# Gate rows of the memory heads by transfers instead of TensorE products, and halves in the first attention

## The chip, the cores and the metric

The kernel runs on one core of a Trainium2 chip. The metric is the device time of one execution in microseconds (us). A core has TensorE (matrix products, PE in the profile), VectorE (DVE), ScalarE (ACT), GpSimd (POOL) and SyncE (SP, here only for transfers). They run side by side and are ordered by semaphores alone.

## The reference, cut to what matters

The program is a small hybrid model (two mixing layers, then a block of two feed-forward parts around a third mixer), for 256 tokens of width 1024, in float32. The change lies in the first layer. It has two branches: four memory heads (mLSTM) and an attention branch (NSA: compressed, selected and windowed keys). Of the memory heads, with `F` the running sum of the log forget gates, `i` the input gate, and `m` the running maximum of `i - F`:

```
a[s] = i[s] - F[s]
m[t] = max(0, max over s <= t of a[s])
S[s,t] = (k[s] . q[t]) * exp(a[s] - m[t])   for s <= t, else 0
h[t] = sum_s S[s,t] v[s] / max(|sum_s S[s,t]|, exp(-(F[t] + m[t])))
```

Each head needs `m[t]` and `F[t]+m[t]`, rows over the tokens `t`, on every one of the 128 partitions, which hold the keys `s`. Tokens are two blocks of 128: the tile for `s` in the first block has 256 columns, that for the second 128, so 384 per head. The attention has two kinds of softmax (`kind` 0 and 1) over the keys, in steps p = 0 to 7, each one block of 128 queries and one pair of heads; p = 4 to 7 have 256 keys.

## The kernel before

Weights come in units of 128 x 1024 numbers through a ring of four slots. SyncE loads a unit, ScalarE copies its high half (`whi`), GpSimd subtracts to get the low half (`wlo`), and TensorE makes 24 products of it (three for each of eight parts: `mm3`). The first layer (`even_in`) goes over 35 units `j`, on each engine in the same order, written out by hand; the small work of the branches stands between units. `ATT_AT` puts attention step `p` at units 18, 19, 20, 21, 22, 23, 25, 27, 28 (p = 0 to 8, where step p does the scores of p and the output of p-1); `ML_AT` puts the memory heads' steps m = 0 to 4 at units 29 to 33. Units 24 and 25, and 26 and 27, are pairs: TensorE does them together, and both end at once.

On ScalarE each unit is: drain of the unit's products where it owns them, `ahead` (wait until the unit is used, then the high half of the unit four later), then the small work. VectorE owns the other drains, and the convolution of units 15 to 22.

The steps that the change touches:

- `masks`: four small constant tiles, `before_bf` among them.
- `gate_maxima` (VectorE, unit 8) leaves `rows4` on four partitions, one for each head: row 2 is `m`, row 3 is `F+m`.
- `mlstm_front(h)` on TensorE: five products that spread the head's rows of `rows4` over all partitions (with a 4 x 128 selector from `pick`) and add 1e30 where `s > t` (with `before_bf`), in PSUM banks 5 and 4; then two query-key products in bank 6. `mlstm(m)` on ScalarE takes three exponentials of them, into `mem` and `mE`; on VectorE, `mlstm(m)` finishes head m-1 (maximum of `mad` and `mem`, reciprocal, product to `hm`) and then weights head m's scores into `mST` (its line in the profile is the helper's). `mlstm_back(h)` on TensorE multiplies `mST` with the values and with ones.
- `scores(p)` on TensorE makes both kinds; `score_maxima` on VectorE; exponentials in `attend` on ScalarE; the weighting of `prob` in `attend` on VectorE; `turned(p, turn)` on TensorE transposes the weights into bank 6, ScalarE copies them to `pt` (`weighted`), and `outputs` uses them. For p >= 4 there are two turns, one for each kind.

The profile shows the helpers' lines: L723 is every product, L2011 and L2020 the two forms of VectorE operations, L1493 every ScalarE function, L1573 the high halves, L658 GpSimd's low halves, L1011 the transposes of `turned`.

Of the kernel before, what the change touches and what calls it, by code (L numbers as in the profile page):

```python
# [16 lines left out]
F32 = mybir.dt.float32  # L17
# [7 lines left out]
P = 128  # L25
# [371 lines left out]
def program(nc, stream, vec_d, row_d, mat_d, cst_d, x_d, out_d):  # L397
    with ExitStack() as ctx:
# [40 lines left out]
        later_bf = sb("later_bf", [P, P], BF16)  # L439
        before_bf = sb("before_bf", [P, P], BF16)  # L440
        notyet_bf = sb("notyet_bf", [P, P], BF16)
# [3 lines left out]


        b1 = ExitStack()
        row = sb("row", [P, NROW], at=b1)
# [39 lines left out]
        flat_rs = rs[:].rearrange("p a b -> p (a b)")  # L488
        mE = flat_rs[:, 0:768].rearrange("p (w t) -> p w t", w=2)
        mST = flat_rs[:, 768:1536].rearrange("p (w t) -> p w t", w=2)  # L490
# [230 lines left out]
        def _(pe):  # L721
# [86 lines left out]
            def even_in():  # L808
# [5 lines left out]
                for j in range(2, E_UNITS):  # L814
# [8 lines left out]
                    if j in ATT_AT:  # L823
                        p = ATT_AT[j]
                        if j in CMP_AT:
                            scores(p)
                            turned(p - 1, 0)
                        else:
                            if p >= 1:
                                turned(p - 1, 0)  # L830
                            if p < 8:
                                scores(p)
                        if p >= 5:
                            turned(p - 1, 1)
                        if p >= 1:
                            outputs(p - 1)
# [86 lines left out]
            def mlstm_front(h):  # L923
                if h == 0:
                    pe.wait_ge(S("row_max"), 3)
                    pe.wait_ge(S("qk_ready"), 2)
                    pe.wait_ge(S("att_pt"), 12)
                else:
                    pe.wait_ge(S("mlstm_st"), h)
                one = C("pick", 512, 4)[:, h * P:(h + 1) * P]  # L930
                mm(ps[:, 5, 0:T], one, rows4[:, 2, :], True, False)
                mm(ps[:, 5, 0:P], ident_bf[:], before_bf[:], False, True)
                mm(ps[:, 5, T:T + P], one, rows4[:, 2, P:T], True, False)
                mm(ps[:, 5, T:T + P], ident_bf[:], before_bf[:], False, True)
                mm(ps[:, 4, 0:T], one, rows4[:, 3, :])
                mm(ps[:, 6, 0:T], qk[:, 4 + h, 0:P], qk[:, h, :])
                mm(ps[:, 6, T:T + P], qk[:, 4 + h, P:T], qk[:, h, P:T]).then_inc(S("mlstm_s"), 1)
# [41 lines left out]

            def scores(p):  # L980
                qt, i = p // 4, p % 4
                nk = P * (qt + 1)
                if p == 0:
                    pe.wait_ge(S("rope_done"), 6)
                    pe.wait_ge(S("masks"), 4)
                else:
                    pe.wait_ge(S("att_exp"), 4 * p)
                for kind in range(2):
                    o = kind * T
                    for g in range(2):  # L990
                        mm(ps[:, 4 + g, o:o + nk], nqk[64 * g:64 * g + 64, i, qt * P:(qt + 1) * P],
                           nqk[64 * g:64 * g + 64, 4 + kind, 0:nk], True, False)
                    for g in range(2):
                        m = mm(ps[:, 4 + g, o + nk - P:o + nk], ident_bf[:], later_bf[:], False, True)
                m.then_inc(S("att_s"), 1)

# [6 lines left out]
            def turned(p, turn):  # L1003
                t = p if p < 4 else 4 + 2 * (p - 4) + turn
                pe.wait_ge(S("att_p"), p + 1)
                if t:
                    pe.wait_ge(S("att_pt"), t)
                if t <= 2:
                    pe.wait_ge(S("cmp_tc"), t // 2 + 1)
                for n, (kind, st, g) in enumerate(blocks(p, turn)):  # L1010
                    m = nc.tensor.transpose(ps[:, 6, n * P:(n + 1) * P],  # L1011
                                            prob[:, p % 2, g, kind * T + st * P:kind * T + (st + 1) * P], C("ident"))
# [476 lines left out]
        def _(act):  # L1489
# [99 lines left out]
            def even_in():  # L1589
# [5 lines left out]
                for j in range(4):  # L1595
                    dst[E_NZ + j] = nz[:, j, :]
                between = {3: (masks,), 5: (forget_log,), 8: (queries_sq,), 10: (queries_rs, hidden), 12: (by_feature,),
                           13: (second_layer, log_table), 14: (kc_rs, gates)}
                for j in range(E_UNITS):
# [17 lines left out]
                    if last:  # L1617
                        weighted(8, 1)
                    elif j in ATT_AT:
                        attend(ATT_AT[j])  # L1620
                    if j == 25:
                        act.wait_ge(S("drained_v"), drained("v", G_E + E_QK + 7))
# [34 lines left out]
            def masks():  # L1657
                act.wait_ge(S("consts_in"), 64)
                func(ident_bf[:], C("ident"), ACT.Copy, "masks")
                func(before_bf[:], C("gt"), ACT.Copy, "masks", scale=BIG)  # L1660
                func(notyet_bf[:], C("nge"), ACT.Copy, "masks", scale=BIG)
# [36 lines left out]
            def forget_log():  # L1698
# [4 lines left out]
                func(ps[:, 7, 64:72], gl[:, 1, :], ACT.Ln, "log1p", bias=eps[:, 2:3])  # L1703

            def log_table():
                nc.scalar.preload_act_table_set(LOG_EXP)
# [6 lines left out]
            def mlstm(m):  # L1713
                if m >= 1:
# [3 lines left out]
                    func(mad[:, (m - 1) % 2, :], ps[:, 7, T:2 * T], ACT.Abs, "mlstm_d")  # L1718
                if m < 4:
                    act.wait_ge(S("mlstm_s"), m + 1)  # L1720
                    if m >= 2:
                        act.wait_ge(S("mlstm_st"), m - 1)
                    func(mem[:, m, :], ps[:, 4, 0:T], ACT.Exp, scale=-1.0)
                    func(mE[:, m % 2, 0:T], ps[:, 5, 0:T], ACT.Exp, scale=-1.0, bias=gl[:, 5, m:m + 1])
                    func(mE[:, m % 2, T:T + P], ps[:, 5, T:T + P], ACT.Exp, "mlstm_e", scale=-1.0,
                         bias=gl[:, 5, 4 + m:5 + m])

            def weighted(p, turn):
                t = p - 1 if p <= 4 else 4 + 2 * (p - 5) + turn
                act.wait_ge(S("att_tr"), t + 1)  # L1730
                if t >= 2:
                    act.wait_ge(S("att_av"), t - 1 if t < 6 else 4 + (t - 4) // 2)
                func(pt[:, t % 2, :], ps[:, 6, :], ACT.Copy, "att_pt")

# [272 lines left out]
        def _(dve):  # L2007
# [97 lines left out]
            def even_in():  # L2105
                between = {4: (small_columns,), 5: (forget,), 6: (gate_columns,), 8: (gate_maxima, compress), 10: (normalized, hidden),
                           11: (rotated,), 14: (kc_n,), 15: (kc_rot,), 18: (compressed,)}
                for j in range(E_UNITS):
# [13 lines left out]
                    if j == 16:  # L2122
                        gated()
                    if j == 27:
                        dve.wait_ge(*once("qk_th"))
# [41 lines left out]
            def gate_maxima():  # L2167
# [3 lines left out]
                step(nc.vector.tensor_tensor_scan(rows4[:, 2, :], rows4[:, 1, :], rows4[:, 1, :], 0.0, ALU.max, ALU.max), "row_max")  # L2171
                tt(rows4[:, 3, :], rows4[:, 2, :], ps[0:4, 4, 0:T], ALU.add, "row_max")

            def normalized():
# [51 lines left out]
            def mlstm(m):  # L2226
# [6 lines left out]
                if m < 4:  # L2233
                    dve.wait_ge(S("mlstm_e"), m + 1)

                    stt(mST[:, m % 2, :], ps[:, 6, 0:384], 0.25 * P ** -0.5, mE[:, m % 2, :], ALU.mult, ALU.mult, "mlstm_st")

# [31 lines left out]
            def attend(p):  # L2269
# [8 lines left out]
                if p < 8:  # L2278
# [5 lines left out]
                    nk = P * (qt + 1)  # L2284
                    weights = prob[:, p % 2].rearrange("p g (k n) -> p (g k) n", k=2)[:, :, 0:nk]
                    tt(weights, weights, end(r, nk), ALU.mult, "att_p")

# [446 lines left out]
```

## Time and profile before

| | us |
|---|---|
| median of 3 runs | 994.34 |
| lowest, highest | 993.43, 994.58 |
| the profiled execution | 993.42 |
| its span in the profile | 991.6 |
| TensorE busy | 938.4 (95%) |
| VectorE busy | 481.5 (49%) |
| ScalarE busy | 535.9 (54%) |
| GpSimd busy | 628.5 (63%) |
| chain that ended last: TensorE's share | 57% |

The span is from the first to the last instruction; the rest of the execution's time lies around it. Busy shares are averages over stages with different limits, so the table of stages and the timelines say more. A row's bracket at its end says how long the engine had stood idle before it and what ended that.

### The profile page before, as it was taken

The page shows a single profiled execution, that of the slowest core. Times are in us where ns is not written, and L with a number is a line of the kernel's source. Part 1 is how long each engine was busy: PE and PEld are TensorE (multiplying, and loading weights), DVE is VectorE, ACT ScalarE, POOL GpSimd, SP SyncE. Part 2 cuts the span into 40 slices and gives each one's busy share as a digit, 9 for nine tenths or more (in the row PEclk, how much of TensorE's full clock was granted, in tenths as well). Part 3 has the DMA queues.
Part 4 walks back from the last instruction along what each step waited for, and adds up shares of the span by engine and source line. Part 5 has one row for each costly group of instructions (what it writes and reads, how often), then busy time and mean ns, then how long its engine had stood idle before and what let it go on. Part 6 is the DMA issues. An engine that isn't in the chain of part 4 may idle for free.

```text
span 991.6 us, 24182 instructions
## 1 busy us (share of the span) xinstructions
PE 938.4 (95%) x9548; PEld 894.6 (90%) x9548; DVE 481.5 (49%) x865; ACT 535.9 (54%) x795; POOL 628.5 (63%) x266
## 2 busy tenths in 40 slices
PE   5999989999888789999999999999999999999997
PEld 4988777899888779999999989999988999999996
DVE  5256534785789764433331133663574743333112
ACT  6577654666945776444443346776322654554441
POOL 2885334377797237977778846654413679788882
PEclk9999999999989999999999999999999999999999
DMA  9644223254434314655555534332002346555551
GB/s 344 205 159 149 73 77 104 67 171 142 159 127 130 128 43 154 210 174 181 172 170 172 180 116 149 128 129 86 3 4 88 118 160 201 183 188 189 180 184 43
DMA packets 39046, 139.86 MB, mean 141 GB/s; under 512 B 4272, under 2 KB 5552, under 8 KB 38832
## 3 DMA queue, kind: packets, MB, share of 16 engines
q1 hardware_dynamic: 38960, 138.62, 42.0%
q8 instruction: 66, 1.08, 0.5%
q14 instruction: 20, 0.16, 0.1%
HBM read 137.55 MB, written 1.05 MB: 140 GB/s over the span
## 4 chain that ended last, share of the span: by engine, by line
PE 57%; issue 9%; DVE 9%; POOL 6%; ACT 4%; POOLq 0%; DVEq 0%; ACTq 0%
PE ps L723 57%; POOL wlo L658 5%; ACT ps L1493 1%; DVE wlo L2011 1%; DVE hA L2439 1%; ACT whi L1573 1%; DVE qkl L2011 1%; DVE ps L2011 1%; POOL rN L699 1%; DVE aL L2020 0%; DVE mad L2011 0%; DVE hT L2047 0%; DVE ivt L2020 0%; POOL dif L682 0%; DVE mixT L2020 0%
## 5 line engine op out<-in xcount | busy, mean ns | idle before, releaser
L658 POOL TENSOR_TENSOR wlo<-ring,whi 128x1024 fp32r<-128x1024 f32 x243 | 585.6, 2424 | 312.7 <-ACT whi L1573 294.6
L1573 ACT ACTIVATE whi<-ring 128x1024 fp32r<-128x1024 f32 x253 | 266.6, 1060 | 204.9 <-PE ps L723 184.7
L723 PE MATMUL ps<-aH,whi 128*128 128x272 f32 (+1 forms) x1048 | 306.6, 293 | 6.1 <-DVE aL L2057 4.9
L723 PE MATMUL ps<-aH,wlo 128*128 128x272 f32 (+1 forms) x1048 | 300.6, 287 | 0.0
L723 PE MATMUL ps<-aL,whi 128*128 128x272 f32 (+1 forms) x1048 | 300.0, 286 | 0.0
L723 PEld LDWEIGHTS ps<-aH,whi 128*128 128x128 f32 x1048 | 199.4, 190 | 11.5 <-DVE wlo L2011 4.8
L723 PEld LDWEIGHTS ps<-aL,whi 128*128 128x128 f32 x1048 | 199.4, 190 | 0.6 <-issue 0.5
L723 PEld LDWEIGHTS ps<-aH,wlo 128*128 128x128 f32 x1048 | 199.4, 190 | 0.0
L723 PE MATMUL ps<-fxH,whi 128*128 128x256 f32 x480 | 135.6, 283 | 3.3 <-DVE fxL L2011 1.8
L723 PE MATMUL ps<-fxL,whi 128*128 128x256 f32 x480 | 135.0, 281 | 0.0
L723 PE MATMUL ps<-fxH,wlo 128*128 128x256 f32 x480 | 135.0, 281 | 0.0
L723 PE MATMUL ps<-fH,wlo 128*128 128x272 f32 (+1 forms) x352 | 100.3, 285 | 0.0
L723 PE MATMUL ps<-fH,whi 128*128 128x272 f32 (+1 forms) x352 | 100.0, 284 | 0.0
L723 PE MATMUL ps<-fL,whi 128*128 128x272 f32 (+1 forms) x352 | 100.0, 284 | 0.0
L723 PEld LDWEIGHTS ps<-fxH,whi 128*128 128x128 f32 x480 | 90.7, 189 | 5.0 <-DVE fxL L2011 2.5
L723 PEld LDWEIGHTS ps<-fxH,wlo 128*128 128x128 f32 x480 | 90.8, 189 | 0.0
L723 PEld LDWEIGHTS ps<-fxL,whi 128*128 128x128 f32 x480 | 90.2, 188 | 0.1
L2011 DVE TENSOR_TENSOR ps<-ps,rstd 128x256 f32<-128x256 f32 (+1 forms) x35 | 15.3, 436 | 113.8 <-PE ps L723 109.4
L723 PEld LDWEIGHTS ps<-fH,whi 128*128 128x128 f32 x352 | 66.3, 188 | 0.0
L723 PEld LDWEIGHTS ps<-fL,whi 128*128 128x128 f32 x352 | 66.2, 188 | 0.0
L723 PEld LDWEIGHTS ps<-fH,wlo 128*128 128x128 f32 x352 | 66.2, 188 | 0.0
L2504 DVE TENSOR_TENSOR ps<-ps,rstd 128x272 f32<-128x272 f32 (+1 forms) x44 | 19.4, 441 | 57.7 <-PE ps L723 48.4
(377 smaller groups left out, 1380.5 us busy)
## 6 DMA issues: line engine op xcount, KB each, us to landing
ring<-in_stream SPq DMA_DIRECT2D x253, 512.0 KB, 3.3
cst<-in_cst SPq DMA_DIRECT2D x1, 1325.0 KB, 12.7
xT<-in_x SPq DMA_DIRECT2D x4, 272.0 KB, 3.5
out<-hT SPq DMA_DIRECT2D x4, 256.0 KB, 2.4
row<-in_row SPq DMA_DIRECT2D x1, 898.0 KB, 9.2
cst<-in_cst SPq DMA_DIRECT2D x1, 640.0 KB, 10.2
mat<-in_mat SPq DMA_DIRECT2D x1, 576.0 KB, 13.5
vec<-in_vec SPq DMA_DIRECT2D x1, 135.0 KB, 3.7
```

The lines of the kernel that those rows point to most:

```text
L658: nc.gpsimd.tensor_tensor(wlo[:, s, :], ring[:, s, :], whi[:, s, :].bitcast(F32), ALU.subtract).then_inc(S("w_split"), 1)
L699: nc.gpsimd.tensor_tensor(rN[:, li % 2], rN0[:], m.unsqueeze(1).broadcast_to([P, 17, 64]), ALU.mult).then_inc(S("r_n"), 1)
L723: return nc.tensor.matmul(out, lhsT, rhs, start=start, stop=stop, skip_group_check=True)
L1493: step(nc.scalar.activation(out, in_, f, **kw), sem)
L1573: nc.scalar.activation(whi[:, v % SLOTS, :], ring[:, v % SLOTS, :], ACT.Copy).then_inc(S("w_high"), 1)
L2011: step(nc.vector.tensor_tensor(out, a, b, op), sem)
L2439: step(nc.vector.copy_predicated(out, m.broadcast_to([P, 8, P // (2 * b), b]).bitcast(U32), src), "lev_a")
L2504: nc.vector.tensor_tensor(gate, gate, rstd[:, 0:TT - c0], ALU.mult).then_inc(S("ffn_gate"), 1)
```

## The change

Row 2 and row 3 of `rows4` are written to a tensor in the chip's memory by one transfer at unit 11, and read back at unit 15 by five transfers that repeat each row on all 128 partitions: into `mE` (now two tiles of two heads each, one in `rs`, one in `mixT`) and `mem`. All six are issued by ScalarE. The 1e30 of the mask is added on VectorE by `masked_rows` at unit 24, for all four heads. The exponentials of `mem` (one for all heads) and of heads 0 and 1 are at unit 26, those of heads 2 and 3 in memory steps 0 and 1. The five gate products of each head go, and `before_bf` with them.

In the attention, steps 5 to 7 make the scores of kind 0, then the first transposes of the step before, then the scores of kind 1. VectorE weights the kinds one after the other for p >= 4, and each turn of transposes waits for its own kind only. The last transposes use bank 4.

```diff
+        rows_d = nc.dram_tensor("gate_rows_d", (4, 2, T), F32).ap()
-        mE = flat_rs[:, 0:768].rearrange("p (w t) -> p w t", w=2)
+        mE = [t[:, 0:768].rearrange("p (w t) -> p w t", w=2) for t in (flat_rs, mixT[:].rearrange("p a b -> p (a b)"))]
...
+                        elif 5 <= p < 8:
+                            scores(p, (0,))
+                            turned(p - 1, 0)
+                            scores(p, (1,))
...
-                one = C("pick", 512, 4)[:, h * P:(h + 1) * P]
-                mm(ps[:, 5, 0:T], one, rows4[:, 2, :], True, False)
-                mm(ps[:, 5, 0:P], ident_bf[:], before_bf[:], False, True)
-                mm(ps[:, 5, T:T + P], one, rows4[:, 2, P:T], True, False)
-                mm(ps[:, 5, T:T + P], ident_bf[:], before_bf[:], False, True)
-                mm(ps[:, 4, 0:T], one, rows4[:, 3, :])
...
-                pe.wait_ge(S("att_p"), p + 1)
-                if t:
+                pe.wait_ge(S("att_p"), t + 1)
+                if t and t < 11:
                     pe.wait_ge(S("att_pt"), t)
...
-                    m = nc.tensor.transpose(ps[:, 6, n * P:(n + 1) * P],
+                    m = nc.tensor.transpose(ps[:, 6 if t < 11 else 4, n * P:(n + 1) * P],
...
+                    if j == 26:
+                        func(mem[:], mem[:], ACT.Exp, scale=-1.0)
+                        for h in range(2):
+                            gate_powers(h)
...
-                func(before_bf[:], C("gt"), ACT.Copy, "masks", scale=BIG)
...
+            def rows_out():
+
+                act.wait_ge(S("row_max"), 3)
+                nc.scalar.dma_start(rows_d, rows4[:, 2:4, :]).then_inc(S("rows_out"), 16)
+
+            def rows_in():
+
+                act.wait_ge(S("rows_out"), 16)
+                def row(what, h0, n, t0):
+                    return rows_d[h0:h0 + n, what, t0:T].unsqueeze(0).broadcast_to([P, n, T - t0])
+                for i in range(2):
+                    nc.scalar.dma_start(mE[i][:, :, 0:T], row(0, 2 * i, 2, 0)).then_inc(S("rows_in"), 16)
+                    nc.scalar.dma_start(mE[i][:, :, T:T + P], row(0, 2 * i, 2, P)).then_inc(S("rows_in"), 16)
+                nc.scalar.dma_start(mem[:], row(1, 0, 4, 0)).then_inc(S("rows_in"), 16)
+
+            def gate_powers(h):
+
+                act.wait_ge(S("rows_masked"), h + 1)
+                e = mE[h // 2][:, h % 2, :]
+                func(e[:, 0:T], e[:, 0:T], ACT.Exp, scale=-1.0, bias=gl[:, 5, h:h + 1])
+                func(e[:, T:T + P], e[:, T:T + P], ACT.Exp, "mlstm_e", scale=-1.0, bias=gl[:, 5, 4 + h:5 + h])
...
-                if m < 4:
-                    act.wait_ge(S("mlstm_s"), m + 1)
-                    if m >= 2:
-                        act.wait_ge(S("mlstm_st"), m - 1)
-                    func(mem[:, m, :], ps[:, 4, 0:T], ACT.Exp, scale=-1.0)
-                    func(mE[:, m % 2, 0:T], ps[:, 5, 0:T], ACT.Exp, scale=-1.0, bias=gl[:, 5, m:m + 1])
-                    func(mE[:, m % 2, T:T + P], ps[:, 5, T:T + P], ACT.Exp, "mlstm_e", scale=-1.0,
-                         bias=gl[:, 5, 4 + m:5 + m])
+                if m < 2:
+                    gate_powers(m + 2)
...
+                    if j == 24:
+                        masked_rows()
...
+            def masked_rows():
+
+                dve.wait_ge(S("rows_in"), 80)
+                for h in range(4):
+                    e = mE[h // 2][:, h % 2, :].rearrange("p (b t) -> p b t", t=P)[:, 0::2, :]
+                    stt(e, mid(C("gt"), 2), BIG, e, ALU.mult, ALU.add, "rows_masked")
...
                     dve.wait_ge(S("mlstm_e"), m + 1)
-
-                    stt(mST[:, m % 2, :], ps[:, 6, 0:384], 0.25 * P ** -0.5, mE[:, m % 2, :], ALU.mult, ALU.mult, "mlstm_st")
+                    dve.wait_ge(S("mlstm_s"), m + 1)
+                    stt(mST[:, m % 2, :], ps[:, 6, 0:384], 0.25 * P ** -0.5, mE[m // 2][:, m % 2, :], ALU.mult, ALU.mult, "mlstm_st")
...
-                    weights = prob[:, p % 2].rearrange("p g (k n) -> p (g k) n", k=2)[:, :, 0:nk]
-                    tt(weights, weights, end(r, nk), ALU.mult, "att_p")
+                    if p < 4:
+                        weights = prob[:, p % 2].rearrange("p g (k n) -> p (g k) n", k=2)[:, :, 0:nk]
+                        tt(weights, weights, end(r, nk), ALU.mult, "att_p")
+                    else:
+                        for kind in range(2):
+                            weights = prob[:, p % 2, :, kind * T:kind * T + nk]
+                            tt(weights, weights, end(r2[:, :, kind], nk), ALU.mult, "att_p")
```

## Rows read from the trace of the kernel before

**Rows 1.** Stages: window, us, then busy us of PE, PEld, DVE, ACT, POOL.
```profile
135.50:161.10 25.60, 23.17 (x207) 18.75 (x205) 10.61 (x17) 15.23 (x29) 11.76 (x5) 1.00 0.27 87
161.10:188.80 27.70, 26.85 (x169) 21.89 (x168) 15.37 (x13) 14.09 (x28) 9.42 (x4) 1.00 0.28 92
```
**Rows 2.** TensorE's timeline, memory heads: start, us, what, idle before.
```profile
161.10 0.69 PE L723 MATMUL ps<-rows,cst 4*128 4x256 f32 x2
...
163.08 0.92 PE L723 MATMUL ps<-qk 128*128 128x256 f32 x4
163.76 0.36 PE L723 MATMUL ps<-aH,whi 128*128 128x256 f32 x1
...
166.64 0.82 PE L723 MATMUL ps<-rs,vtok 128*128 128x256 f32 x4
...
174.06 0.92 PE L723 MATMUL ps<-rs,vtok 128*128 128x256 f32 x4 [0.30 <-DVE rs L2020]
...
188.84 0.92 PE L723 MATMUL ps<-rs,vtok 128*128 128x256 f32 x4 [0.59 <-DVE rs L2020]
```
**Rows 3.** ScalarE's timeline, memory heads.
```profile
164.46 0.88 ACT L1493 ACTIVATE rs<-ps,gl 128x256 f32<-128x256 f32 x2
```
**Rows 4.** VectorE's timeline, memory heads.
```profile
168.84 2.33 DVE L2011 TENSOR_TENSOR mad<-mad,mem 128x256 f32<-128x256 f32 x1 [2.85 <-ACT mad L1493]
...
192.75 0.42 DVE L2011 TENSOR_TENSOR mad<-mad,mem 128x256 f32<-128x256 f32 x1
```
**Rows 5.** GpSimd's timeline, attention and memory heads.
```profile
136.90 4.70 POOL L658 TENSOR_TENSOR wlo<-ring,whi 128x1024 fp32r<-128x1024 f32 x2 [9.01 <-ACT whi L1573]
...
168.54 2.35 POOL L658 TENSOR_TENSOR wlo<-ring,whi 128x1024 fp32r<-128x1024 f32 x1 [3.25 <-ACT whi L1573]
```
**Rows 6.** L2020 by operands (minimum/median/maximum ns), and VectorE's timeline.
```profile
L2020 DVE SCALAR_TENSOR_TENSOR fQ<-fQ,mixT x5: 424/426/1812, 262.3 to 268.6; 128x256 f32<-128x256 f32 x5
...
84.93 1.52 DVE L2020 SCALAR_TENSOR_TENSOR qk<-ps,vec,qk 128x253 f32<-128x253 f32 x3
86.48 1.41 DVE L2020 SCALAR_TENSOR_TENSOR nz<-th,nz 128x1024 f32<-128x1024 f32 x1
```
**Rows 7.** TensorE's timeline, attention.
```profile
95.74 1.05 PE L977 MATMUL ps<-cst,pc 128*15 128x128 f32 x8 [2.30 <-DVE pc L2011]
...
125.60 0.66 PE L1011 MATMUL ps<-cst,prob 128*128 128x128 f32 x4 [1.80 <-DVE prob L2011]
...
127.04 0.70 PE L723 MATMUL ps<-nqk 64*128 64x256 f32 x4
...
149.01 0.63 PE L1011 MATMUL ps<-cst,prob 128*128 128x128 f32 x4 [0.58 <-ACT pt L1493]
```
**Rows 8.** VectorE's timeline, attention.
```profile
90.94 1.78 DVE L2011 TENSOR_TENSOR pc<-pc,cs 128x240 f32<-128x240 f32 x1
...
124.32 1.22 DVE L2011 TENSOR_TENSOR prob<-prob,pst 128x1024 f32<-128x1024 f32 x1
...
135.78 0.89 DVE L2011 TENSOR_TENSOR vtok<-ps,row 128x256 f32<-128x256 f32 x2 [2.30 <-PE ps L723]
137.92 1.22 DVE L2267 TENSOR_REDUCE pst<-ps 128x4 f32<-128x1024 f32 x1 [1.25 <-PE ps L723]
```
**Rows 9.** ScalarE's timeline, attention.
```profile
81.86 0.43 ACT L1493 ACTIVATE ps<-ps,vec 128x256 f32<-128x256 f32 x1
...
142.13 1.92 ACT L1493 ACTIVATE th<-qk 128x2048 f32<-128x2048 f32 x1
146.38 2.00 ACT L1573 ACTIVATE whi<-ring 128x1024 fp32r<-128x1024 f32 x2 [2.33 <-PE ps L723]
148.29 0.58 ACT L1493 ACTIVATE pt<-ps 128x512 f32<-128x512 f32 x1
...
150.36 0.47 ACT L1493 ACTIVATE prob<-ps,pst 128x256 f32<-128x256 f32 x1
```
**Rows 10.** SyncE's timeline: DMA issues at the start.
```profile
0.75 1.82 SPq L616 DMA_DIRECT2D xT<-in_x  x4
```

More of the change, by code:

```diff
@@ L439, in program @@
         later_bf = sb("later_bf", [P, P], BF16)
-        before_bf = sb("before_bf", [P, P], BF16)
         notyet_bf = sb("notyet_bf", [P, P], BF16)
@@ L924, in mlstm_front @@
                 if h == 0:
-                    pe.wait_ge(S("row_max"), 3)
                     pe.wait_ge(S("qk_ready"), 2)
@@ L978, in compressed_rows, with scores @@
                 m.then_inc(S("cmp_t"), 1)
-            def scores(p):
+            def scores(p, kinds=(0, 1)):
                 qt, i = p // 4, p % 4
@@ L984, in scores @@
                     pe.wait_ge(S("rope_done"), 6)
-                    pe.wait_ge(S("masks"), 4)
+                    pe.wait_ge(S("masks"), 3)
                 else:
                     pe.wait_ge(S("att_exp"), 4 * p)
-                for kind in range(2):
+                for kind in kinds:
                     o = kind * T
@@ L994, in scores @@
                         m = mm(ps[:, 4 + g, o + nk - P:o + nk], ident_bf[:], later_bf[:], False, True)
-                m.then_inc(S("att_s"), 1)
+                if kinds[-1] == 1:
+                    m.then_inc(S("att_s"), 1)
             def blocks(p, turn):
@@ L1597, in even_in @@
                 between = {3: (masks,), 5: (forget_log,), 8: (queries_sq,), 10: (queries_rs, hidden), 12: (by_feature,),
-                           13: (second_layer, log_table), 14: (kc_rs, gates)}
+                           13: (second_layer, log_table), 14: (kc_rs, gates), 11: (rows_out,), 15: (rows_in,)}
                 for j in range(E_UNITS):
@@ L1732, in weighted @@
                     act.wait_ge(S("att_av"), t - 1 if t < 6 else 4 + (t - 4) // 2)
-                func(pt[:, t % 2, :], ps[:, 6, :], ACT.Copy, "att_pt")
+                func(pt[:, t % 2, :], ps[:, 6 if t < 11 else 4, :], ACT.Copy, "att_pt")
             def attend(p):
```

## The prediction

> **What bounds the kernel now.** I read the table of stages first, then TensorE's own timeline in the two stages that the change touches, then ScalarE, VectorE and GpSimd in the same stretches. TensorE is busy nearly all the time, so a removed product is worth something only if nothing else then becomes late. The table shows two places that matter: attention, from 135.50 to 161.10, where TensorE is busy 23.17 of 25.60 us, and the memory heads, 161.10 to 188.80, 26.85 of 27.70 us [rows 1]. Outside the first layer nothing is edited, and the weight ring has only four slots, so time gained or lost here is neither stored nor spent later: the layer's change is the kernel's change.
>
> In the memory stage the reader is to see a loop. For each head TensorE does one front (gate products and query-key products), one projection unit and the back of the head before. One front runs from 161.10 to 163.76, of which the part before 163.08 (1.98 us) is the five gate products; the unit runs from 163.76 to 166.64 [rows 2]. Beside it runs a chain through ScalarE, VectorE and back: ScalarE's absolute value, the maximum at 168.84 (2.33 us), then 2.9 us for reciprocal, product and weighting, and the next back at 174.06 [rows 2, 4]. TensorE waits only 0.30 and 0.59 us at the backs of 174.06 and 188.84 [rows 2]: chain and products are almost equally long.
>
> The 2.33 us of that maximum is not its work: the same 256 columns take 0.42 us at 192.75 [rows 4]. GpSimd's subtraction runs from 168.54 for 2.35 us, and the maximum ends as it ends [rows 4, 5]. VectorE operations with two operands in SBUF stand still behind a GpSimd subtraction that began earlier. fQ's row says the same: 424 ns at best, 1812 at worst for one shape, an addition-and-product form (the one that masked_rows uses) [rows 6]. The Trainium skill (SBUF — State Buffer, "Who interferes with whom") says that a VectorE instruction with two SBUF inputs and a GpSimd one that reads SBUF exclude each other for the whole instruction. By that rule, the trace agrees.
>
> **Memory stage.** Removed: five gate products in each of four heads, 4 x 1.98 = 7.9 us of TensorE [rows 2]; three exponentials per head move out of the loop, two of them (0.88 us, [rows 3]) staying at heads 2 and 3. If TensorE alone set the pace, the gain would be 7.9. It doesn't. Count from the first front, F = 161.10. The front is now 0.68, the unit 2.88, so the unit ends at F+3.56. ScalarE does drain, high half and absolute value behind it as before; from the unit's end (166.64) to the next back (174.06) the old trace takes 7.42 us [rows 2], because GpSimd's subtraction again comes 0.3 us before the maximum. Back 1: F+10.98 (before F+12.96).
> Next head: that back takes 1.5 (1.40 from 166.64 to the front behind it, and a restart after the wait), the front 0.68, the unit ends at F+16.04. GpSimd's subtraction was started by the unit that ended at F+8.52; with the 1.90 us between 166.64 and 168.54 [rows 2, 5] it runs F+10.4 to 12.75, and the maximum asks 0.6 after the back's end, at F+13.06: free, 0.42 instead of 2.33. Then 2.9: back 2 at F+16.38, with TensorE idle 0.3.
> Third: the subtraction F+17.9 to 20.3 comes before the maximum's request at F+18.46, so it is blocked again: back 3 at F+23.46, against 188.84 - 161.10 = 27.74 before [rows 2]. Gain 4.3 us; the rest of the 7.9 turns into waits of TensorE at backs 1, 2, 3 of some 2.4, 0.3 and 2.0 us, where it waited 0.30 and 0.59 before. Bounds: 7.9 if the chain were never in the way; 2.4 if the second maximum is blocked too (1.9 more). I take 4.3, the count from the rows. What follows (four low halves, the last head, squares) keeps its distance from back 3 to 0.2 us.
>
> **First split head (p=5).** Before, transposes at 125.60 waited 1.80 for the weights [rows 7]. The weighting started 124.32 and took 1.22 in one [rows 8]; in halves the first is done 0.53 sooner. The first kind of the next scores now lies in the wait; before, it ran behind the transposes, which with it take 1.44, 0.66 of them the transposes [rows 7], so 0.8 is hidden. Sum: 1.3 us sooner. At p=6 and 7 TensorE does not wait for the weights, so the split gives nothing; at p=8 the next transpose goes to a free bank, but ScalarE's high half still lies between its two copies: 0.05.
>
> **masked_rows at p=6.** It stands on VectorE behind the pair's drain (135.78 + 0.89 = 136.67) and ahead of the score maximum that started at 137.92 [rows 8]. Four additions over two SBUF operands, 256 columns each, some 0.45 with the gap (fQ's 424 ns, [rows 6]). The first is in before GpSimd's subtractions (136.90, two in 4.70 [rows 5]). The second waits out one subtraction, the third the other, since each side gets the port when the other's instruction ends. Relative to U = 135.51: done at U+7.6 instead of U+3.1. The score maximum goes from U+2.4 to U+7.6, the exponentials end at U+11.3.
> Behind them on ScalarE are the tanh of 2048 columns (1.92, [rows 9]), then the high half at 146.38, and now, before the next high half and before the copy that the transposes of p=7 wait for (149.01, [rows 7]), the new exponentials: one of 1024 columns (1.0, half of the tanh's 2048) and two pairs at 0.88 [rows 3], with gaps 2.9 us. The copy, before at 148.29, comes at U+18.15; the second transposes at U+18.85 (before U+13.5); then the exponentials of p=7 at U+20.2, before 150.36 = U+14.85 [rows 9]: 5.35 later. The first half of the weights gives 0.55 back, and attention ends 4.8 later, net of the 1.3 above 3.5. Bounds: 0 if ScalarE hid everything (excluded: the copy is in order behind them and TensorE already waits 0.58 for it [rows 7]); 2.3 if the additions never stand behind GpSimd; 4.8. I take 4.8, since rows 4 and 6 both show the block.
>
> **The transfers (j=11 and 15).** One write and five broadcasts, all issued by ScalarE. The trace has no issue from ScalarE; on SyncE four take 1.82, 0.46 each [rows 10]. Five are 2.3 to 3.0 us, during which ScalarE's next bias (81.86, [rows 9]) waits; the high half at 80.89 covers 0.96. So it is 1.4 to 2.0 late. VectorE takes that unit at 84.93 [rows 6], 2.05 us after ScalarE has it ready (a scaling of like width behind the bias), which would hide it, but the high half behind it is late too, so GpSimd's subtraction now starts at about 85.7 and stands before the gate product at 86.48, which in this trace slipped in between two of them [rows 6]. I get 1.1 to 1.9 later at the subtraction of 90.94, on which TensorE waits 2.30 at 95.74 [rows 8, 7]. Bounds: 0 (issues under 0.2 us, or over 0.52, where the product again comes first) and 1.9. I take 1.5. The data are 1.3 MB in a stretch where the transfer engines are not the limit and are wanted 50 us later: nothing. The write at j=11 lies in a wait of ScalarE; one mask copy less at j=3 as well: nothing, and TensorE has no wait there.
> The Trainium skill (DMA: Bandwidth & Descriptors, "Issuing engines are not separate DMA queues") calls the issue time on the sequencer usually small relative to the transfer. Read as nothing, that gives a sum 1.5 lower. Here SyncE's rows show 0.46 for a 512 KB load that lands in 3.3, small but not free.
>
> **Sum.** -4.3 (memory) -1.3 (p=5) +4.8 (p=6, 7) +1.5 (issues) = +0.7, less 0.05: +0.6 us. The profiled run was 993.42 (span 991.6, 1.8 around it), 0.9 under the median of 994.34; the change is taken on the median: 994.9.
>
> **Rivals.**
> 1. The additions of masked_rows do not stand behind GpSimd. For: only some of the two-operand rows are slow. Against: rows 4 and 6. Then -1.9 us; 992.5, just at the bound of 0.2%. With issues free as well -3.4: 991.0.
> 2. The memory loop is not held by the maximum, because a shift of 0.5 us makes VectorE's request come first at back 3 or at back 1. Each takes 1.9 off: one gives -1.3, both -3.2 (991.1). For: requests are only 0.3 and 0.5 us apart. Against: at 168.84 the order is set by one engine, ScalarE's high half, then its absolute value.
> 3. Slower: ScalarE's issues are dear. The broadcasts have 256 to 512 rows each. From 1.2 us each (6.0 in all), ScalarE is 5.0 late, 3.0 beyond the cover of 2.05, and the compressed scores with it: +3.0 in place of 1.5, sum +2.1, 996.4; at 1.5 us each +3.6. Against: SyncE's 0.46. That the second maximum is blocked too (+1.9, sum +2.5) ends on the same side.
> 4. The change does not do what it says: the products are gone for certain; only their worth is in question.
>
> **Chances.** Forecast: 0.38, within 0.2% (2.0 us, about what a measurement of this kernel can tell from no change). Rival 1: 0.22, of which 0.12 beyond that bound (with cheap issues). Rival 2: 0.18, of which 0.12 beyond (both backs). Rival 3 with its companion: 0.22, all slower. So faster 0.24, same 0.38 + 0.10 + 0.06 = 0.54, slower 0.22. The range is from 990.8 (rivals 1 or 2 at their best) to 997.3 (rival 3 between 1.2 and 1.5 us).
>
> **What would show it.** In the changed profile: backs of the memory heads 5.4 to 7.4 us apart, maxima of 2.3, 0.42, 2.3 us, and TensorE waits of about 2 us for VectorE; masked_rows' additions of 2 us and more, and the score maximum of p=6 some 5 us later in its unit; a TensorE wait of about 4 us (not 0.58) for the pt copy in p=7; the wait of 1.80 in p=5 gone; the wait of 2.30 at the compressed rows grown to about 3.8. I am wrong if the additions take 0.5 each, if the copy in p=7 is on time, or if three maxima of 0.42 follow each other.

## The result and the profile after

The changed kernel takes 999.85 us (median of 6 runs, 997.05 to 1002.62), the kernel before, run beside it, 994.03 (992.07 to 994.75). The ratio is 1.0060, with a 95% interval of 1.0041 to 1.0078: slower by 5.8 us, outside the range of 990.8 to 997.3. The profiled execution is one of the fastest (997.05, span 995.2); its mean granted clock is 0.984, against 0.992 before. It is only 3.6 us longer than the profiled execution of the kernel before (993.42), where the medians are 5.8 apart; the two traces speak for the first of these differences.

TensorE's timeline of the changed kernel (the rows that answer to [rows 2, 7]):

```profile
97.70 1.05 PE L974 MATMUL ps<-cst,pc 128*15 128x128 f32 x8 [2.10 <-DVE pc L2028]
...
127.06 0.66 PE L1009 MATMUL ps<-cst,prob 128*128 128x128 f32 x4 [0.29 <-DVE prob L2028]
...
136.32 0.70 PE L723 MATMUL ps<-nqk 64*128 64x256 f32 x4
...
154.67 1.09 PE L1009 MATMUL ps<-cst,prob 128*128 128x128 f32 x4 [4.88 <-ACT pt L1491]
...
169.38 0.82 PE L723 MATMUL ps<-qk 128*128 128x256 f32 x4
...
180.35 0.92 PE L723 MATMUL ps<-rs,vtok 128*128 128x256 f32 x4 [2.51 <-DVE rs L2037]
...
185.77 0.92 PE L723 MATMUL ps<-rs,vtok 128*128 128x256 f32 x4 [0.34 <-DVE rs L2037]
...
192.72 1.53 PE L723 MATMUL ps<-rs,vtok 128*128 128x256 f32 x4 [1.88 <-DVE rs L2037]
```

Apart from the first row, the waits are where the prediction put them. But the duration in the second column is to be read too: the four transposes at 154.67 take 1.09 us where those of 149.01 took 0.63 [rows 7], and the back at 192.72 takes 1.53 where that of 188.84 took 0.92 [rows 2]. The same instructions run slower. The table of windows (us; busy us of PE, PEld, DVE, ACT, POOL; then TensorE's granted clock) says why; first the kernel before, then the changed one:

```profile
152.00:162.00 10.00, 8.73 (x74) 7.14 (x73) 4.31 (x6) 4.00 (x10) 2.58 (x2) 1.00 0.37 123
```

```profile
152.00:162.00 10.00, 7.33 (x41) 6.37 (x42) 3.22 (x6) 5.30 (x13) 2.84 (x2) 0.50 0.35 107
162.00:169.00 7.00, 6.07 (x57) 5.25 (x57) 1.54 (x3) 2.61 (x4) 2.37 (x1) 0.99 0.04 4
...
192.70:196.00 3.30, 3.28 (x12) 2.93 (x13) 3.23 (x3) 0.40 (x2) 2.22 (x1) 0.53 0.02 5
```

For ten microseconds TensorE was granted half its speed: 0.50 is the lower of its two levels, 1.2 GHz in place of 2.4. Before that it had stood still for 4.88 us. At the third back, behind waits of 2.51, 0.34 and 1.88 us, a shorter slow stretch comes (0.53).

A third slow stretch is hidden; it is the first in time. The wait at the compressed rows was to grow from 2.30 to about 3.8 and is 2.10, though the rows themselves are late. The products ahead of it ran slowly, so TensorE came late too; the same table, one microsecond to the row:

```profile
89.00:90.00 1.00, 1.00 (x18) 1.00 (x17) 0.96 (x2) 0.97 (x2) 1.00 (x1) 1.00 1.05 392
...
91.00:92.00 1.00, 1.00 (x9) 0.78 (x8) 0.90 (x4) 0.00 (x0) 1.00 (x1) 0.50 0.74 291
92.00:93.00 1.00, 1.00 (x6) 1.00 (x6) 0.90 (x4) 0.00 (x0) 1.00 (x2) 0.50 0.21 86
```

The last product ahead of the wait begins at 95.31 here and at 93.16 before: 2.15 later, of which 0.67 came with it. Without the slow stretch the wait would have been 3.6. This one cost nothing, because TensorE had to wait for VectorE there anyway, and the stage behind it is as long as in the kernel with the attention's halves alone, where no such stretch lies ahead (38.6 us from the compressed rows to the first product behind the pair before p=6).

Reading off when the same piece of work starts in both traces gives the ledger. The shift of a row is its start after less its start before; the last column is what the stage added.

| up to | before | after | shift | this stage | forecast |
|---|---|---|---|---|---|
| ScalarE's high half ahead of the issues | 80.89 | 81.56 | +0.67 | +0.67 | 0 |
| compressed rows | 95.74 | 97.70 | +1.96 | +1.29 | +1.5 |
| first product behind the pair before p=6 | 135.51 | 136.32 | +0.81 | -1.15 | -1.3 |
| first memory front | 161.10 | 169.38 | +8.28 | +7.47 | +4.8 |
| third back | 188.84 | 192.72 | +3.88 | -4.40 | -4.3 |
| sums of squares of the next norm | 224.95 | 230.46 | +5.51 | +1.63 | 0 |
| end of the span | 991.6 | 995.2 | +3.6 | -1.9 | 0 |

The first line isn't the work of the transfers: the kernel with the attention's halves alone, which changes nothing ahead of that row, has it at 81.42. The last line lies in code that the change does not touch, and is the clock's for the most part: the kernel before has slow stretches there for some 13.6 us in all (an estimate from rows of 1 us: at 272, 336 and 603 us), the changed kernel for some 10.2 (at 278 and 329), which is up to 1.7 us of work.

VectorE and GpSimd at unit 24, where masked_rows stands (they answer to [rows 5, 8]):

```profile
136.50 0.88 DVE L2028 TENSOR_TENSOR vtok<-ps,row 128x256 f32<-128x256 f32 x2 [2.22 <-PE ps L723]
137.42 2.92 DVE L2037 SCALAR_TENSOR_TENSOR rs<-cst,rs 128x256 f32<-128x256 f32 x2
140.37 2.95 DVE L2037 SCALAR_TENSOR_TENSOR mixT<-cst,mixT 128x256 f32<-128x256 f32 x2
143.36 1.22 DVE L2293 TENSOR_REDUCE pst<-ps 128x4 f32<-128x1024 f32 x1
...
137.62 4.96 POOL L658 TENSOR_TENSOR wlo<-ring,whi 128x1024 fp32r<-128x1024 f32 x2 [7.67 <-ACT whi L1571]
```

Four additions take 5.9 us; away from GpSimd's subtractions they take 1.8 (the second experiment below). The score maximum comes 7.04 after the pair's end (136.32) instead of 2.41. ScalarE behind it:

```profile
147.06 1.91 ACT L1491 ACTIVATE th<-qk 128x2048 f32<-128x2048 f32 x1
149.00 1.06 ACT L1571 ACTIVATE whi<-ring 128x1024 fp32r<-128x1024 f32 x1
149.97 1.04 ACT L1491 ACTIVATE mem<-mem 128x1024 f32<-128x1024 f32 x1
151.04 1.92 ACT L1491 ACTIVATE rs<-rs,gl 128x256 f32<-128x256 f32 x4
152.99 1.06 ACT L1571 ACTIVATE whi<-ring 128x1024 fp32r<-128x1024 f32 x1
153.95 0.58 ACT L1491 ACTIVATE pt<-ps 128x512 f32<-128x512 f32 x1
```

The copy to pt comes at 153.95, 17.63 after the pair's end (counted: 18.15). And the five issues on ScalarE's queue, after which its next bias starts at 84.20, not 81.86 [rows 9]:

```profile
81.57 0.40 ACTq L1717 DMA_DIRECT2D rs<-gate_rows_d  x1
82.00 0.48 ACTq L1718 DMA_DIRECT2D rs<-gate_rows_d  x1
82.51 0.60 ACTq L1717 DMA_DIRECT2D mixT<-gate_rows_d  x1
83.14 0.49 ACTq L1718 DMA_DIRECT2D mixT<-gate_rows_d  x1
83.66 0.49 ACTq L1719 DMA_DIRECT2D mem<-gate_rows_d  x1
84.20 0.45 ACT L1491 ACTIVATE ps<-ps,vec 128x256 f32<-128x256 f32 x1 [1.57 <-issue]
```

The product on nz, 1.41 us before [rows 6], now stands behind a subtraction for 2.73 us (start 87.14).

In the memory heads, VectorE's three maxima (they answer to [rows 4]) are blocked, free and blocked, as forecast:

```profile
175.08 2.38 DVE L2028 TENSOR_TENSOR mad<-mad,mem 128x256 f32<-128x256 f32 x1 [4.18 <-ACT mad L1491]
...
182.45 0.43 DVE L2028 TENSOR_TENSOR mad<-mad,mem 128x256 f32<-128x256 f32 x1 [2.15 <-ACT mad L1491]
...
187.87 1.96 DVE L2028 TENSOR_TENSOR mad<-mad,mem 128x256 f32<-128x256 f32 x1 [2.15 <-ACT mad L1491]
```

### The profile page after: what moved, and what is told of

Read it like the earlier page. It is cut to its first block, busy times and chain, and to the rows that moved or that the text cites. A ratio compares the mean times of both kernels' runs of the same rounds, so it can differ in the third digit from the quotient of the medians.

```text
span 995.2 us, 24128 instructions
## 1 busy us (share of the span) xinstructions
PE 934.6 (94%) x9516; PEld 893.6 (90%) x9516; DVE 489.3 (49%) x873; ACT 534.9 (54%) x791; POOL 627.8 (63%) x266
## 4 chain that ended last, share of the span: by engine, by line
PE 57%; issue 9%; DVE 8%; POOL 6%; ACT 4%; POOLq 0%; ACTq 0%; DVEq 0%
PE ps L723 57%; POOL wlo L658 5%; ACT ps L1491 1%; DVE wlo L2028 1%; ACT whi L1571 1%; DVE hA L2470 1%; DVE mad L2257 1%; POOL rN L699 0%; DVE qkl L2028 0%; DVE aL L2037 0%; DVE ps L2028 0%; DVE mad L2028 0%; DVE hT L2064 0%; DVE ivt L2037 0%; POOL dif L682 0%
```

## The experiments

Every time is compared with runs of the kernel before on the same chip, so ratios are compared with ratios; the changed kernel's own, 1.0060, is the mark.

**Is the loss the clock's? TensorE kept at work in p=7.**

```diff
+                            if p == 7:
+                                for _ in range(7):
+                                    mm(ps[:, 0, 0:432], C("ones"), cst[:, 0:432])
```

> The changed kernel with seven products of 432 columns (about 0.7 us each, result unused, into a free bank) put into TensorE's stream at p=7, where it otherwise stands still for 4.88 us. No other work moves. Clock theory: TensorE is granted half speed from about 151 to 162 because it stood still; kept at work it keeps full speed, the outputs of p=6, unit 28 and the last transposes take their old times, and the time falls by 2 to 3 us (to about 997). Queue theory (the loss is only the late copy from ScalarE): the fillers end when the copy comes, nothing changes, 999.9, within 0.5.

Measured: 995.85 us (10 runs), ratio 1.0023 (1.0004 to 1.0042), some 3.7 us less than the changed kernel's ratio gives. Added work made the kernel faster. TensorE's timeline of this kernel:

```profile
152.96 5.29 PE L723 MATMUL ps<-cst 128*128 128x432 f32 x14
158.09 0.60 PE L1012 MATMUL ps<-cst,prob 128*128 128x128 f32 x4
158.98 1.10 PE L723 MATMUL ps<-pt,vsw 128*64 128x128 f32 x16
```

Its windows:

```profile
158.00:170.00 12.00, 11.29 (x104) 9.57 (x104) 4.75 (x8) 5.69 (x14) 4.73 (x2) 1.00 0.22 74
...
97.00:101.00 4.00, 3.50 (x18) 2.17 (x18) 3.68 (x9) 2.73 (x6) 0.00 (x0) 0.53 0.00 1
101.00:104.00 3.00, 2.93 (x20) 1.85 (x18) 1.34 (x3) 2.10 (x6) 2.34 (x1) 0.50 0.00 0
```

The copy still comes late (157.28, which is 17.62 after the pair's end at 139.66; 17.63 in the changed kernel), but behind it the transposes take 0.60 and the outputs 1.10, at a granted clock of 1.00. From the pair's end to the first memory front it is now 29.86 us, against 33.06 in the changed kernel and 25.59 before. So the clock costs 3.2 us in this stage, and all the rest of the change 4.27. In this execution a slow stretch lies at 97 to 104 us, where the changed kernel's trace shows 1.00 on the same code: how an execution is clocked there varies. The waits at the backs are as in the changed kernel (2.51, 0.35 and 1.88 us), but the third back takes 0.92 and no slow stretch follows; from there to the sums of squares it is 36.16 us, as before (36.11), against 37.74 in the changed kernel.

**Each suspected place by itself.** masked_rows at unit 21, the exponentials at unit 28, the issues at unit 18:

```diff
-                    if j == 24:
+                    if j == 21:
                         masked_rows()
```

> The changed kernel with masked_rows at the end of unit 21 instead of unit 24, where VectorE has 1.8 us without work and GpSimd rests. If the additions behind GpSimd's subtractions make p=6 late: they take 0.45 each, the score maximum of p=6 comes 5.2 us earlier, TensorE's wait in p=7 falls from 4.88 to about 3.5 us (ScalarE's exponentials at unit 26 remain), a gain of 2 to 2.4 us, and up to 2.7 more if the shorter wait keeps the clock. If ScalarE's exponentials alone hold p=7, the wait stays near 4.9 and the gain is under 0.5.

```diff
-                    if j == 26:
+                    if j == 28:
+                        act.wait_ge(S("rows_in"), 80)
                         func(mem[:], mem[:], ACT.Exp, scale=-1.0)
                         for h in range(2):
                             gate_powers(h)
```

> The changed kernel with the exponentials of mem and of heads 0 and 1 at the end of unit 28 instead of unit 26, in a stretch where ScalarE waits 3.8 us. masked_rows stays at unit 24. If the exponentials in the queue before the copy cost what I counted: TensorE's wait in p=7 falls from 4.88 to about 2.1 us, a gain of 2.6 to 2.9 us, and up to 2.7 more with the clock. If the late score maximum alone holds p=7: the wait stays, gain under 0.5.

```diff
-                           13: (second_layer, log_table), 14: (kc_rs, gates), 11: (rows_out,), 15: (rows_in,)}
+                           13: (second_layer, log_table), 14: (kc_rs, gates), 11: (rows_out,), 18: (rows_in,)}
```

> The changed kernel with the five broadcast transfers issued at unit 18 instead of unit 15, where ScalarE waits 3.6 us for VectorE. If the issues delay GpSimd's subtraction and with it the product on nz (2.73 us instead of 1.41) and the compressed scores: 1.2 us less before 97.7, time 1.2 lower, unless a slow stretch of the clock moves. If the issues were covered: no change, within 0.5.

Measured: 998.94 (ratio 1.0057, 1.0037 to 1.0077), 996.10 (1.0024, 1.0012 to 1.0036) and 996.97 (1.0037, 1.0025 to 1.0049). The waits in TensorE's timelines, first with masked_rows at unit 21, then with the exponentials at 28, then with the issues at 18:

```profile
153.66 1.09 PE L1009 MATMUL ps<-cst,prob 128*128 128x128 f32 x4 [3.61 <-ACT pt L1491]
```

```profile
151.20 0.92 PE L1009 MATMUL ps<-cst,prob 128*128 128x128 f32 x4 [1.84 <-ACT pt L1491]
```

```profile
96.36 1.04 PE L974 MATMUL ps<-cst,pc 128*15 128x128 f32 x8 [0.76 <-DVE pc L2028]
```

The waits moved as counted: 4.88 to 3.61 and to 1.84 in p=7, and 2.10 to 0.76 at the compressed rows. The additions at unit 21 took 0.89 and 0.88 us for two each. The times did not follow the waits one to one. With masked_rows early the ratio falls by 0.0003 only, where 2 us (0.0020) were expected: the two intervals are wide enough for that, but my number missed. Its trace shows where the gain went. From the pair's end (137.25) to the first memory front (167.66) it is 2.6 us shorter than in the changed kernel, somewhat more than expected, though the transposes after the wait of 3.61 us are still slow (1.09). But from there to the third back it is 24.92 us instead of 23.34: a slow stretch at 180 to 184 (granted clock 0.58) lies behind the first back, and the third waits 2.49 us. With the exponentials at 28 the gain is 3.6 us by the ratios. The clock falls there behind a wait of only 1.84 us (transposes 0.92, granted clock 0.53 from 151 to 158), for a shorter time. The issues at 18 gave 2.3 us by the ratios where 1.2 was due; the product on nz is back at 1.41 us.

**Both places of the attention, then the issues too.** The first kernel has masked_rows at 21 and the exponentials at 28, the second has the issues at 18 as well:

> masked_rows at unit 21 and the three exponential groups at unit 28 together. If these two places are all that the attention loses: TensorE's wait in p=7 is back at 0.6 us, no slow stretch of the clock follows it, the first memory front comes 7.5 us earlier than in the changed kernel relative to p=5, the memory heads keep their gain of 4.4, and the time is 990 to 991.5, some 3 us under the kernel before. If a third thing holds p=7, a wait of over 1.5 us stays and the time is over 993.

> As the one before, with the five transfers issued at unit 18 as well. My count gives 1.3 us less than with the issues at unit 15 (wait at the compressed rows 0.76 instead of 2.1), 989 to 990. A rival that says the early stage is hidden in the end gives no difference between the two.

Measured: 992.90 (0.9993, 0.9978 to 1.0007) and 989.63 (0.9951, 0.9936 to 0.9967). The wait in p=7 is 0.57 us in both, as before the change, and the transposes after it take 0.63: no third thing holds p=7. But the first is 1.5 to 3 us over what I expected, and TensorE's timeline of it shows one reason in the memory heads:

```profile
173.01 1.65 PE L723 MATMUL ps<-rs,vtok 128*128 128x256 f32 x4 [2.51 <-DVE rs L2038]
...
186.91 0.92 PE L723 MATMUL ps<-rs,vtok 128*128 128x256 f32 x4 [2.06 <-DVE rs L2038]
```

The back after 2.51 us of standing still takes 1.65 instead of 0.92. The second kernel has the time that was expected. Its profiled execution is the slowest of its eight (994.07), and the wait at the compressed rows is 2.27 there, not 0.76: no slow stretch lies ahead of it (1.00 from 90 to 94), and one lies behind it (0.52 from 97 to 107).

**The maximum behind GpSimd.** The absolute value goes to PSUM, so the maximum has one operand in SBUF. Once on top of the kernel before this one, once alone on the changed kernel:

```diff
-                    func(mad[:, (m - 1) % 2, :], ps[:, 7, T:2 * T], ACT.Abs, "mlstm_d")
+                    func(ps[:, 5, (m - 1) % 2 * T:(m - 1) % 2 * T + T], ps[:, 7, T:2 * T], ACT.Abs, "mlstm_d")
...
-                    tt(d, d, mem[:, m - 1, :], ALU.max)
+                    tt(d, ps[:, 5, (m - 1) % 2 * T:(m - 1) % 2 * T + T], mem[:, m - 1, :], ALU.max)
```

> As the one before, and ScalarE writes the absolute value of each head's denominator into PSUM (bank 5, now free) instead of SBUF, so that VectorE's maximum has only one operand in SBUF. If the maximum of 2.33 us is a wait for GpSimd's subtraction, it takes 0.45 in every head, TensorE's waits of 2.5 and 1.9 us at backs 1 and 3 fall below 0.6, the rest of the 7.9 us comes in (3 to 3.5 more), no slow stretch of the clock follows, and the time is 985 to 987. If VectorE's chain is long for another reason, the maximum stays at 2.3 and the time stays at 989 to 990.

> The changed kernel with nothing but the absolute value in PSUM. If the maximum behind GpSimd's subtraction is what ate the rest of the 7.9 us in the memory heads: backs 5.4 us apart throughout, 3 to 3.5 us less, and up to 1.7 more because the slow stretch that follows the wait at back 3 is not entered: 995 to 997 against 999.9. p=7 keeps its wait of 4.9 and its slow stretch. If the lock is not it: 999.9.

Measured: 983.76 (4 runs; 0.9907, 0.9875 to 0.9938) and 994.30 (12 runs; 0.9998, 0.9986 to 1.0011). VectorE's and TensorE's timelines of the kernel with all four edits:

```profile
165.27 0.43 DVE L2029 TENSOR_TENSOR mad<-ps,mem 128x256 f32<-128x256 f32 x1 [4.19 <-ACT ps L1491]
...
170.68 0.42 DVE L2029 TENSOR_TENSOR mad<-ps,mem 128x256 f32<-128x256 f32 x1 [2.14 <-ACT ps L1491]
...
176.08 0.43 DVE L2029 TENSOR_TENSOR mad<-ps,mem 128x256 f32<-128x256 f32 x1 [2.14 <-ACT ps L1491]
```

```profile
168.59 0.92 PE L723 MATMUL ps<-rs,vtok 128*128 128x256 f32 x4 [0.56 <-DVE rs L2038]
173.99 0.92 PE L723 MATMUL ps<-rs,vtok 128*128 128x256 f32 x4 [0.33 <-DVE rs L2038]
179.39 0.92 PE L723 MATMUL ps<-rs,vtok 128*128 128x256 f32 x4 [0.33 <-DVE rs L2038]
```

And one of GpSimd's subtractions in it:

```profile
164.97 2.40 POOL L658 TENSOR_TENSOR wlo<-ring,whi 128x1024 fp32r<-128x1024 f32 x1 [1.11 <-ACT whi L1571]
```

Three maxima of 0.42 to 0.43, backs 5.4 apart, TensorE waiting 0.3 to 0.6 us. Each maximum begins and ends inside a subtraction (the other two start at 169.77 and 175.40), and none is held by it. The wait of 2.33 us was GpSimd's. Alone on the changed kernel the edit gives 5.5 us by the medians and 6.2 by the ratios, though its trace has p=7 unmended (wait 4.88, transposes 1.09); 3.5 of them were counted as the waits that vanish. The slow stretch at the third back, which cost the changed kernel 1.6 us (the tail's line in the ledger), does not occur in this trace: its granted clock from 163 to 196 us is 1.00. But one trace doesn't stand for twelve runs. Their mean granted clock is 0.983, the same as that of the changed kernel's six, so the clock as a whole was no better, and 2 to 2.7 us of this gain stay unexplained.

**The two parts of the change.** The kernel before with the halves alone, and the best kernel without the halves:

> The kernel before with only the attention part of the change (scores and weights of p=4 to 7 in halves, last transposes in bank 4). My count: the wait of 1.80 us at p=5 shrinks to 0.3, 1.2 us less, nothing elsewhere: 992.3 against 993.6. Rival, that the halves lose their gain at the next ScalarE copies: within 0.3 of the kernel before.

> The best kernel so far (gate rows by transfers, issues at unit 18, masked_rows at unit 21, exponentials at unit 28, maximum from PSUM) without the attention's halves. The halves alone gave 2.7 us on the kernel before, where my count says 1.2. If the parts add: 985 to 986.5 against 983.8. If the halves' gain was partly chance of the clock: 984.5 to 985.

Measured: 990.97 (10 runs; 0.9969, 0.9954 to 0.9983) and 985.63 (0.9919, 0.9905 to 0.9932). The halves are worth 3.1 us on the kernel before (2.7 by the medians) and, by the ratios, 1.2 on the best kernel, of which four runs leave an interval of some 3 us either way. In both the wait at p=5 is what changes (1.80 to 0.29, and 1.91 to 0.28), 1.5 us. The rest of the 3.1 isn't in any stage of the first layer's timeline. The mean granted clock of the ten runs is 0.993, against 0.9915 in the 23 runs of the kernel before beside them; the difference is up to 1.4 us of TensorE's work (0.0014 of 990 us, an estimate), about what is missing. Whether the halves bring that about or chance does isn't shown. The gate rows with their three mended places and the maximum are worth 0.81%, 8 us.

**The control: stand still without the change.** On the kernel before, four exponentials whose result nobody uses, ahead of the copy in p=7; then the same with six unused products on TensorE:

```diff
+                    if j == 26:
+                        for _ in range(4):
+                            func(mem[:], nz[:], ACT.Exp, scale=-1.0)
```

```diff
+                        if p == 7:
+                            for _ in range(6):
+                                mm(ps[:, 0, 0:432], C("ones"), cst[:, 0:432])
```

> The kernel before with four exponentials of 1024 columns (about 1.07 us each, result unused) on ScalarE at unit 26, ahead of the copy that the second transposes of p=7 wait for. It lengthens that wait of TensorE from 0.58 to about 4.9 us and changes nothing else. Queue alone: 3.8 to 4.3 us slower, 997.4 to 998. Clock theory: in most executions a slow stretch of 3.4 to 10.2 us follows as well, 1.7 to 5 us more: 999 to 1001.

> The same, with six products of 432 columns (about 0.7 us each, result unused) in TensorE's stream where it would stand still. Queue alone: the same time as without them, within 0.5. Clock theory: no slow stretch after p=7, 1.5 to 3 us faster than without them, 997 to 998.

Measured: 1001.98 (1.0082, 1.0065 to 1.0099) and 997.02 (1.0036, 1.0023 to 1.0049), 5 us apart. TensorE's timeline and one row of the windows of the first:

```profile
153.49 1.09 PE L1011 MATMUL ps<-cst,prob 128*128 128x128 f32 x4 [4.93 <-ACT pt L1493]
```

```profile
156.00:160.00 4.00, 4.00 (x26) 3.67 (x23) 2.44 (x5) 1.58 (x6) 0.00 (x0) 0.51 0.41 135
```

And of the second:

```profile
148.48 4.57 PE L723 MATMUL ps<-cst 128*128 128x432 f32 x12
153.58 0.63 PE L1014 MATMUL ps<-cst,prob 128*128 128x128 f32 x4 [0.53 <-ACT pt L1496]
```

```profile
156.00:160.00 4.00, 3.26 (x27) 2.82 (x25) 2.52 (x5) 1.87 (x7) 0.00 (x0) 1.00 0.38 131
```

The copy comes equally late in both (transposes at 153.49 and 153.58). What differs is whether TensorE stood still in front of it. Against the kernel before, a copy that comes 4.4 us later costs 3 to 3.6 us where TensorE is kept at work, and 4.6 to 5 more where it stands still (by the ratios and by the medians). That is more than the 1.5 to 3 expected. The two traces show 3.8 of it: from these transposes to the first memory front's query-key products the first kernel takes 2.2 us longer, and from there to the first back 1.6, in a second slow stretch (0.50 at 171 to 173) ahead of which TensorE had stood still for no more than 0.91 us. Whether the first stretch brings on the second isn't shown.

## Why the prediction was wrong

The list of mechanisms was right and most of their sizes were. What was missing is a term.

- Memory heads, "gain 4.3": measured 4.40, with backs at F+10.97, 16.39 and 23.34 against 10.98, 16.38 and 23.46 counted, and maxima blocked, free, blocked.
- p=5, "1.3 us sooner": 1.15. Transfers, "I take 1.5": 1.29, from five issues of 0.40 to 0.60 us. The sign that I gave for it, the wait "grown to about 3.8", did not show, because TensorE came late for the reason told above. Rival 3 (dear issues) falls with these rows.
- masked_rows behind GpSimd: 5.9 us for the four additions against 6.4 counted (1.2 to 7.6); rival 1 falls. The copy in p=7 came 17.63 after the pair's end, counted 18.15.
- The step that failed is the sum of that part, "attention ends 4.8 later": it is 7.47. The copy came even earlier than counted; what follows it was costed at durations from full clock, and between 152 and 162 TensorE ran at half. With the clock kept by unused products the same part is 4.27, so the queues were even a little overcounted (by 0.5) and the clock's term, put at nothing, is 3.2. The prediction had noted a wait of over 4 us on TensorE and asked only what was late next, not what it does to TensorE's own speed. The same omission stands in "keeps its distance from back 3 to 0.2 us": measured 1.63 more, after the waits that the prediction itself had listed (2.4, 0.3, 2.0). Together 4.3 us are missing (2.67 and 1.63): with them the sum of +0.6 is +4.9, near the measured 5.8 (+5.51 in the traces, up to the next norm).
- That idleness is the cause is shown for p=7, the larger part: the unused products take the slow stretch away in the changed kernel (1.0060 to 1.0023) and in the control (1.0082 to 1.0036), with the copy as late as without them. For the 1.63 behind the third back it isn't shown. The slow stretch is seen there, but in two other traces the same waits (2.51, 0.34 or 0.35, and 1.88 us) are followed by full clock (unused products in p=7, and exponentials at unit 28), and nobody kept TensorE at work at the backs.
- The range was made from queue effects of both signs and could not hold this: a cost that only adds, wherever a gap on TensorE is long.

The record gives the mean granted clock of every run. Within a kernel, the runs with the lower clock are by and large the longer ones. A thousandth of it is 2 us at half speed, so up to 1 us of TensorE's work (an estimate).

| kernel | runs | mean granted clock |
|---|---|---|
| before (three groups) | 25, 23, 20 | 0.991 to 0.992 |
| changed | 6 | 0.983 (slowest run 0.978, the two fastest 0.984 and 0.987) |
| changed, unused products in p=7 | 10 | 0.989 |
| changed, masked_rows at 21 | 5 | 0.981 |
| both places moved | 10 | 0.985 |
| maximum from PSUM alone on the changed kernel | 12 | 0.983 |
| all four edits | 4 | 0.990 |
| before with the halves alone | 10 | 0.993 |
| before, copy late | 6 | 0.986 |
| before, copy late, unused products | 8 | 0.992 |

What stays open: what starts the slow stretches in the first layer that no wait of 3.6 us or more precedes (90, 97, 170 to 190 us), and those behind it (270 to 340, 600 us), where the waits weren't looked at; and how often each comes, since there is one profile for each kernel. With them stay open why the changed kernel with masked_rows early has the lowest clock of all, 2 to 2.7 us of what the maximum from PSUM gave alone, and half of what the halves gave.

## What to carry to other kernels

When products leave TensorE, ask how long TensorE stands still in the place, not only what the chain costs: a gap of nearly five microseconds was paid twice here, and unused products in the gap gave the second payment back. Work moved to another engine must be put where that engine waits, seen in its own timeline, and not between a copy and the transposes that need it; the same work at units 18, 21 and 28 turned a loss of 0.6% into a gain of 0.5%. An operand moved to PSUM took VectorE out of GpSimd's way and made the removed products count: 0.9% faster than the kernel before, 983.8 us against 993.7.

## What the runs showed of the hardware

- After TensorE had stood still for 4.88 us its granted clock was 0.50 from 152 to 162 us, and the same four transposes took 1.09 us, not 0.63. After waits of 1.8 to 2.5 us it sometimes fell and sometimes did not: the back after 2.51 us took 0.92 at 180.35 in the changed kernel and 1.65 at 173.01 in the kernel with both places moved, and after 1.84 us in p=7 it was 0.53 from 151 to 158 us in the kernel with the exponentials at unit 28. The Trainium skill (TensorE: Matmul & The Clock Gate, "What's actually happening") says that the gate in front of the array's clock is set by how busy TensorE has been lately, so idling is paid again as a slower restart. By that rule, the control pair agrees: same late copy, slow without the unused products, fast with them. The next item does not follow from it.
- The clock also fell with no wait ahead of it. From 90.5 to 93.7 us it was 0.50 in the changed kernel, behind some thirty products of 15 columns each, with TensorE shown as busy throughout; the kernel before ran the same products and kept 1.00. This isn't chance alone: nine of the ten traces with transferred rows have a slow stretch there (not the one with both places and the issues moved), and none of the four without. What causes it wasn't tested.
- A scalar-tensor-tensor of 256 columns with both operands in SBUF took 0.44 us with GpSimd at rest and some 1.5 on average while GpSimd ran two subtractions (5.9 us for four). A maximum of 256 columns with one operand in PSUM took 0.42 to 0.43 us inside a subtraction; with both in SBUF it took 1.96 to 2.38 when the subtraction had begun first.
- A broadcast of 256 to 512 rows of 512 to 1024 bytes took 0.40 to 0.60 us of ScalarE's queue to issue (0.49 on average; SyncE's four loads took 0.46 each), and landed 4.7 to 7.5 us later.
